# Dilated heads of a hybrid attention layer: gated results written over their gates, and the first head's operands loaded during the phase before

## What is computed

```python
h = layer_norm(x, ln0_g, ln0_b)
proj = jnp.einsum('btd,dc->btc', h, w_in[l])
qa, ka, va, qb, kb, vb, gate = jnp.split(proj, split_at, axis=-1)
ya = dilated_mixture(heads_a(qa), heads_a(ka), heads_a(va), rel_bias).reshape(b, t, WIDTH_A)
yb = stick_breaking(heads_b(qb), heads_b(kb), heads_b(vb)).reshape(b, t, WIDTH_B)
y = jnp.concatenate([ya, yb], axis=-1) * jax.nn.silu(gate)
out = jnp.einsum('btc,cd->btd', y, w_out[l]) + b_out[l]
h = layer_norm(DEEPNORM_ALPHA * h + out, ln_g[l], ln_b[l])
```

## Time and profile before

| what | value |
|---|---|
| median of 3 runs | 1833.44 us |
| the three runs | 1833.44, 1836.2, 1826.37 us |
| profiled execution | 1834.93 us |
| its span in the profile | 1833.1 us |
| TensorE busy | 1706.5 us, 93% |
| VectorE busy | 1173.7 us, 64% |
| ScalarE busy | 806.1 us, 44% |
| GpSimd busy | 194.7 us, 11% |
| mean granted TensorE clock | 0.967 |

### The profile page before, as it was taken

The page is one execution under the profiler, slowest core; times in us unless marked ns, Lnnn a source line. Parts: engine busy times, 40 slices in busy tenths (PEclk is TensorE's granted clock), DMA queues, the critical chain, the costliest instruction groups (busy, mean ns, idle before and its releaser), DMA issues. The chain is left out here.

```text
span 1833.1 us, 27600 instructions
## 1 busy us (share of the span) xinstructions
PE 1706.5 (93%) x9138; PEld 1457.2 (79%) x9138; DVE 1173.7 (64%) x2323; ACT 806.1 (44%) x1993; POOL 194.7 (11%) x172
## 2 busy tenths in 40 slices
PE   5799999999979999999999999959989899959998
PEld 4577888888868888888787888849989899947886
DVE  5531123333238888888888888837667676765996
ACT  3341112222225555555555555538768686742000
POOL 2102100000000000000000000010222222200231
PEclk9899999999989999999999999979989999979999
DMA  4316954666367539465654454259888888446541
GB/s 161 138 66 222 333 193 166 208 200 209 131 188 221 179 124 289 141 179 177 228 178 150 144 157 153 89 140 204 191 213 180 198 183 195 106 135 216 187 151 59
DMA packets 235236, 320.01 MB, mean 175 GB/s; under 512 B 66781, under 2 KB 160408, under 8 KB 231516
## 3 DMA queue, kind: packets, MB, share of 16 engines
q1 hardware_dynamic: 230620, 308.90, 56.5%
q0 software_dynamic: 2400, 9.48, 1.6%
q10 hardware_dynamic: 2080, 0.01, 0.1%
HBM read 208.38 MB, written 109.94 MB: 174 GB/s over the span
## 5 line engine op out<-in xcount | busy, mean ns | idle before, releaser
L1003 ACT ACTIVATE WT_hi<-wt_ps 128x512 fp32r<-128x512 f32 (+1 forms) x320 | 170.9, 534 | 316.3 <-PE wt_ps L935 316.3
L1049 DVE TENSOR_TENSOR_SCAN W<-w,W,zeros 128x512 f32<-128x512 f32 x192 | 248.2, 1293 | 59.3 <-ACT w L995 58.5
L376 PE MATMUL proj<-h_hi,w_hi 128*128 128x512 f32 x640 | 260.2, 407 | 19.2 <-DVE h_lo L552 16.5
L376 PE MATMUL proj<-h_hi,w_lo 128*128 128x512 f32 x640 | 253.2, 396 | 0.0
L376 PE MATMUL proj<-h_lo,w_hi 128*128 128x512 f32 x640 | 252.9, 395 | 0.0
L1358 ACT ACTIVATE prob<-neg_s,rows 128x256 f32<-128x256 f32 (+1 forms) x384 | 173.5, 454 | 51.8 <-DVE rows L1418 47.9
L1057 DVE TENSOR_TENSOR WT_lo<-wt_ps,WT_hi 128x512 fp32r<-128x512 f32 (+1 forms) x320 | 187.4, 586 | 2.2 <-ACT WT_hi L1003 2.2
L1294 PE MATMUL s_ps<-k_both,q_hi 128*128 128x256 f32 (+1 forms) x384 | 151.9, 402 | 38.1 <-DMA q_lo<-qk_lo_d 20.1
L1418 DVE CUSTOM_DVE_ANT_0 neg_s<-s_ps,bias 128x256 f32<-128x256 f32 (+1 forms) x384 | 122.6, 363 | 99.5 <-PE s_ps L1295 89.3
L935 PE MATMUL wt_ps<-ident,W 128*128 128x128 f32 x1088 | 173.5, 275 | 7.0 <-DVE WT_lo L1057 6.2
L995 ACT ACTIVATE w<-z_ps 128x512 f32<-128x512 f32 (+2 forms) x320 | 169.3, 529 | 19.4 <-PE z_ps L925 19.4
(11 more groups left out here) (134 smaller groups left out, 3355.4 us busy)
## 6 DMA issues: line engine op xcount, KB each, us to landing
wa_hi<-wa_d SPq DMA_DIRECT2D x48, 512.0 KB, 3.9
wa_lo<-wa_d SPq DMA_DIRECT2D x48, 512.0 KB, 5.0
va<-va_d SPq DMA_DIRECT2D x32, 512.0 KB, 11.4
wa_d<-x_sb SPq DMA_DIRECT2D x24, 512.0 KB, 3.8
w_raw<-in_w_tiles SPq DMA_DIRECT2D x18, 512.0 KB, 5.1
moved<-move_d SPq DMA_DIRECT2D x16, 528.0 KB, 4.2
x_sb<-in_x SPq DMA_DIRECT2D x16, 512.0 KB, 5.9
qk_hi_d<-st SPq DMA_DIRECT2D x32, 256.0 KB, 2.8
```

What stands on the lines that cost most here:

```text
L376: last = pe.matmul(acc[n % ACC_SLOTS][:], w[w_slot(t)][:, k, :], h[ch][:, k, :], start=(k, a) == (0, 0), stop=(k, a) == (KD - 1, 2))
L1003: act.activation(WT_hi[n % PART_SLOTS][:, cols], t_ps[n % T_SLOTS][:, cols], ACT.Copy) \
L1049: dve.tensor_tensor_scan(W[n % W_SLOTS][:, 0:width][:, ::-1], w[n % W_IN][:, 0:width][:, ::-1], above[:, ::-1], first, ALU.mult, ALU.max). ...
```

## The change

Three things.

1. **Gates.** `apply_gate` writes its product over the gate that it read (`gate`, one tile of 128 x 2048), and the ring `ya_out` is gone, with VectorE's wait on `y_stored`. SP's `finish` stores from `gate`, and now waits until all four stores have landed, before `load_gate` overwrites the tile.
2. **First head.** The tiles of parity 0 of `HeadTiles` (queries, keys, bias) become views of `h_hi[0]` and `h_lo[0]`, for the whole dilated phase. Head 0's queries, keys and bias are loaded in the stick phase: columns 0 to 1535 and the bias at steps 244 and 246, six and eight steps after the last group of chunk 2, and columns 1536 to 2047 at step 281, eight steps after the group of head 0's keys in chunk 3. GpSimd clears the lower half of that `q_lo` in the stick phase as well; the one of parity 1 stays in the dilated phase.
3. **The end of the stick phase.** SP no longer waits there for its stores. It issues head 0's values first in the dilated phase, and waits for the stores after that, before head 1's loads.

```diff
-    def __init__(self, nc, stack):
+    def __init__(self, nc, stack, h_hi, h_lo):
         m = Memory(nc, stack)
-        self.k_both = m.ring("k_both", 2, [P, T], F32R)
...
+        hi, lo = h_hi[:].rearrange("p k c -> p (k c)"), h_lo[:].rearrange("p k c -> p (k c)")
+        self.k_both, self.q_hi2, self.q_lo0 = [hi[:, 0:T]], [hi[:, T:2 * T]], [lo[:, 0:T]]
+        self.bias = [lo[:, T:T + 6 * P].bitcast(F32).rearrange("p (c u) -> p c u", c=3)]
...
+    def set_zeros(self, pool, par):
+        pool.memset(self.q_lo0[par][DH:P, :].bitcast(F32), 0.0).then_inc(self.zeros_set, 1)
...
@@ stick phase, sync
+            def load_first(upto):
+                cols = slice(0, T - CH) if upto < NCH else slice(T - CH, T)
+                stored = A_TILES * (upto - 1) + 4
+                sp.wait_ge(a_done, A_TILES * (NCH - 1))
+                sp.wait_ge(a_stored[stored % 2], a_stored_by(stored))
+                heads.load_qk(sp, qk_hi_d, qk_lo_d, 0, 0, heads.first_loaded, cols)
...
+            plan(A_END[A_TILES * (NCH - 1) - 1] + 6, load_first, NCH - 1)
+            plan(A_END[A_TILES * (NCH - 1) - 1] + 8, load_first_bias)
+            plan(A_END[A_TILES * (NCH - 1) + 4] + 8, load_first, NCH)
...
-            for slot in range(2):
-                sp.wait_ge(y_stored[slot], 16 * GROUPS // 2)
-                sp.wait_ge(a_stored[slot], a_stored_by(A_GROUPS - 2 + slot))
@@ dilated phase, sync
                     sp.dma_start(y_d[bass.ds(pair * P, P), ch * CH:(ch + 1) * CH],
-                                 y_out[ch % 2][:]).then_inc(y_stored[ch % 2], 16)
+                                 gate[:, ch * CH:(ch + 1) * CH]).then_inc(y_stored, 16)
+                sp.wait_ge(y_stored, at(pair, 16 * NCH, 16 * NCH))
...
-            heads.load_dilated(sp, qk_hi_d, qk_lo_d, toe_d, 0, 0)
             load_values(0, 0)
-            heads.load_dilated(sp, qk_hi_d, qk_lo_d, toe_d, 1, 1)
+            for slot in range(2):
+                sp.wait_ge(a_stored[slot], all_stored[slot])
+                sp.wait_ge(b_stored[slot], all_y_stored[slot])
+            heads.load_qk(sp, qk_hi_d, qk_lo_d, 1, 1, qk_loaded[1])
+            heads.load_bias(sp, toe_d, 1, 1)
@@ dilated phase, vector
-                dve.wait_ge(y_stored[ch % 2], at(pair, 16 * NCH // 2, 16 * (ch // 2 + 1)))
-                dve.tensor_tensor(y_out[ch % 2][:], y_ps[ch % 2][:], gate[:, ch * CH:(ch + 1) * CH],
-                                  ALU.mult).then_inc(gated, 1)
+                cols = gate[:, ch * CH:(ch + 1) * CH]
+                dve.tensor_tensor(cols, y_ps[ch % 2][:], cols, ALU.mult).then_inc(gated, 1)
@@ dilated phase, gpsimd
-            for par in range(2):
-                pool.memset(q_lo0[par][DH:P, :].bitcast(F32), 0.0).then_inc(q_zeros_set, 1)
             pool.sem_inc(merged, 1)
+            heads.set_zeros(pool, 1)
```

More of the change, by code:

```diff
@@ L653, in __init__ @@
         self.qk_loaded, self.bias_loaded = m.sems("a_qk_loaded", 2), m.sems("bias_loaded", 2)
[L655 to L665, removed]
+        self.first_loaded, self.zeros_set = m.sem("a_first_loaded"), m.sem("a_q_zeros_set")
@@ new lines, in add_odd, with load_qk @@
+    def add_odd(self, nc, stack):
+        m = Memory(nc, stack)
+        for tiles, name in ((self.k_both, "k_both"), (self.q_hi2, "q_hi2"), (self.q_lo0, "q_lo0")):
+            tiles.append(m.sb(name, [P, T], F32R)[:])
+        self.bias.append(m.sb("bias", [P, 3, 2 * P])[:])
+    def set_zeros(self, pool, par):
+        pool.memset(self.q_lo0[par][DH:P, :].bitcast(F32), 0.0).then_inc(self.zeros_set, 1)
+    def load_qk(self, sp, qk_hi_d, qk_lo_d, head, par, loaded, cols=slice(0, T)):
+        q, k = head * DH, head * DH + WIDTH
+        for tile, half, src, row in ((self.k_both, 0, qk_hi_d, k), (self.k_both, DH, qk_lo_d, k),
+                                     (self.q_hi2, 0, qk_hi_d, q), (self.q_hi2, DH, qk_hi_d, q),
+                                     (self.q_lo0, 0, qk_lo_d, q)):
+            sp.dma_start(tile[par][half:half + DH, cols].bitcast(F32), src[bass.ds(row, DH), cols]) \
+                .then_inc(loaded, 16)
@@ L666, in load_dilated, with load_bias @@
+    def load_bias(self, sp, toe_d, head, par):
         for c in range(3):
@@ L725, in stick_phase @@
     A_END = [next(s for s in range(STEPS) if DEALT[s] >= (a + 1) * KD * 3) for a in range(A_GROUPS)]
+    FIRST_FREE = next(n for n in range(GROUPS) if LAST[n] > A_END[A_TILES * (NCH - 1) - 1])
     def a_group(a):
@@ L844, in store_a, with load_first_bias @@
                     sp.dma_start(gate_d[row:row + P, cols], lo).then_inc(a_stored[a % 2], 16)
+            def load_first(upto):
[4 more added lines that the diff above has]
+                heads.load_qk(sp, qk_hi_d, qk_lo_d, 0, 0, heads.first_loaded, cols)
+            def load_first_bias():
+                heads.load_bias(sp, toe_d, 0, 0)
             later = {}
@@ L906, in _ @@
             for n in range(GROUPS):
+                if n == FIRST_FREE:
+                    pool.wait_ge(a_done, A_TILES * (NCH - 1))
+                    heads.set_zeros(pool, 0)
                 pool.wait_ge(gate_loaded[n % 2], 16 * (n // 2 + 1))
@@ L1090, in _, with dilated_phase @@
                     add_halves(LAST.index(s - VALUES_LAG - 1))
-def dilated_phase(nc, qk_hi_d, qk_lo_d, gate_d, va_d, toe_d, ident, y_d):
+    return [a_stored_by(A_GROUPS - 2 + slot) for slot in range(2)], [16 * GROUPS // 2] * 2
+def dilated_phase(nc, heads, a_stored, all_stored, b_stored, all_y_stored, qk_hi_d, qk_lo_d, gate_d, va_d, toe_d, ident, y_d):
     TURN_HEADS = 2
@@ L1154, in dilated_phase @@
         m = Memory(nc, stack)
-        heads = HeadTiles(nc, stack)
+        heads.add_odd(nc, stack)
         k_both, q_hi2, q_lo0, bias = heads.k_both, heads.q_hi2, heads.q_lo0, heads.bias
@@ L1264, in _ @@
                     sp.wait_ge(rows_done, 2 + at(it, 2 * OBANKS, (par + 1) * OBANKS))
-                    heads.load_dilated(sp, qk_hi_d, qk_lo_d, toe_d, at(it, 2, 2 + par), par)
+                    heads.load_qk(sp, qk_hi_d, qk_lo_d, at(it, 2, 2 + par), par, qk_loaded[par])
+                    heads.load_bias(sp, toe_d, at(it, 2, 2 + par), par)
                     load_values(at(it, 2, 2 + par), par)
@@ L1271, in _ @@
             finish(PAIRS - 1)
-            for i in range(2):
-                sp.wait_ge(y_stored[i], 16 + 16 * PAIRS * NCH // 2)
         @block.tensor
@@ L1284, in scores @@
                 if b % NB == 0:
-                    pe.wait_ge(qk_loaded[par], at(it, 16 * HeadTiles.QK_LOADS, 16 * HeadTiles.QK_LOADS))
+                    first = isinstance(it, int) and it == 0
+                    if first:
+                        pe.wait_ge(heads.zeros_set, par + 1)
+                    if first and par == 0:
+                        pe.wait_ge(heads.first_loaded, 16 * HeadTiles.FIRST_LOADS)
+                    else:
+                        pe.wait_ge(qk_loaded[par], at(it, 16 * HeadTiles.QK_LOADS, 16 * HeadTiles.QK_LOADS * par))
                 pe.wait_ge(min_done, at(it, STEPS, b + 1))
@@ L1795, in build @@
         rstd = stack.enter_context(nc.sbuf_tensor("rstd", [P, TB], F32))
[L1796 to L1804, removed]
```

38 lines of the change are left out of this document (25 added, 13 removed).

## The result

| what | before | changed |
|---|---|---|
| median | 1834.63 us (7 runs) | 1817.92 us (7 runs, 1814.99 to 1825.96) |
| ratio | | 0.9928, 95% interval 0.9912 to 0.9945 |
| profiled execution, its span | 1834.93, 1833.1 us | 1825.96, 1824.1 us |
| mean granted TensorE clock | 0.967 | 0.956 |

The change is faster by 13 us by the ratio and 16.7 by the medians, where 25.5 were forecast. That is the right sign, but between half and two thirds of the size. The median of 1817.9 us lies just inside the range of 1799 to 1819; by the ratio (0.9928 x 1833.4 = 1820 us) it is just outside. The profiled execution is the slowest of the seven; a second profile is with the experiments (e10).

What follows compares the result with a forecast made beforehand. TensorE, busy 93% of the span, was taken as the bound, so only its waits could be won. Start 16.1 plus gatings 9.4 gave 25.5 us off 1834.9, 1809.4 profiled, stated as 1808 us median, range 1799 to 1819.

Steps and rivals of the forecast that it cites:

- The start: Start of the dilated phase: SP's store wait and head 0's loads leave the path, giving 16.1 us.
- the forecast's lower bound: Start of the dilated phase: only 13 us gained if the clock or the order of transfers gives 3 back.
- The moved wait: VectorE's store wait at the gating moves eleven steps on, to the moved rows: 5.0 us at head 2, 4.4 at head 4.
- the 0.8 us of the forecast: SP's chain at the gating: earlier gate load and late stores no longer running against it, together worth 0.8 us.
- The 46.8 us for an undisturbed stretch: Between heads with a gating and no wait: 44.0 us plus some 2.8 for transposes and products.
- the three gatings: Gating of three pairs: 13.3 us won before the clock's charge of 3.9, 9.4 us after it.
- The stick phase: Early loads ahead of group 38's weights: cost 0 within 10 us of slack, 5 us as the other bound.
- I charge 1.3 us behind each of the three moved waits: Lower TensorE clock behind the waits for moved rows: 3.9 us in all, taken from head 0's 1.84 us wait.
- The rule from the Trainium skill: TensorE's lower clock: half the time at it, 3.5 us per wait, 10.5 for three; set aside for 1.3 each.
- All of both waits goes: Rival: SP's chain comes in time, gatings give 26.6 us, total gain 42.7, so 1791 us; chance 0.15.
- Only the start gives: Rival: SP's new wait delays gate load and moves, the clock takes the rest, so 1816 us; chance 0.18.
- The slower rival: SP's wait for all four stores delays each turn; needs a landing 17 us after issue; 1853 us at 20; chance 0.02.

Runs made afterwards that it cites:

- e10: The changed kernel run once more, unaltered, for a second profile: 1822.78 us, ratio 0.9936.
- e2: The changed kernel with the old result ring and old waits for stores, keeping head 0's early loads: 1819.97 us, ratio 0.9921.
- e5: e3 with the loop over turns written out on TensorE, ScalarE and VectorE: 1786.47 us, ratio 0.9747.
- e1: The kernel before with only the gates written over and SP's wait for the four stores: 1843.0 us, ratio 1.0040.
- e6: The changed kernel with the loop over turns written out on TensorE, ScalarE and VectorE: 1820.45 us, ratio 0.9926.
- e7: e5 with eight idle VectorE additions at step 24 of turns 1 to 3, where weigh_maxima stands: 1818.96 us, ratio 0.9922.
- e3: The changed kernel with gate load and SP's wait for stores moved behind head 0's moves in the turn using the gate: 1792.24 us, ratio 0.9759.
- e9: e1 with gate load and SP's wait for stores behind head 0's moves, no early first head: 1803.99 us, ratio 0.9841.
- e8: e5 with eight idle VectorE additions at step 13 of turns 1 to 3, ahead of the gating: 1814.33 us, ratio 0.9886.
- e4: The changed kernel with 24 extra TensorE transposes at step 26 of each turn, result unused: 1823.66 us, ratio 0.9929.

## Why the prediction was right and wrong

*The start: right, with some luck in the number.* First scores came at 1209.9 (1211.1 forecast) and the rows of head 0 were used at 1269.3 (1269.4), 16.3 us against 16.1, behind a wait of 3.0 us. But e10 has 13.1 us at this station, without a wait, and e2 12.8. That is the forecast's lower bound, and its condition, time given back by the clock, is what e10 shows. Counted up to head 1, e10 is 14.4 us ahead and the first profile 11.5.

*The moved wait: right in kind, and mostly in place.* Waits stand at heads 0, 2 and 4 in the first profile (3.0, 4.7, 4.3 us) and at heads 2, 4 and 6 in e10 (5.2, 5.0, 3.9). Forecast were 1.84 us for head 0 and 5.0, 4.4 and about as long for the other three (3.6 for head 6 by the same sum, which the prediction did not work out). So each profile has one fewer than was forecast. From the first store of a pair to the next gate load is 9.6 us, 1340.12 to 1349.73, where it was 10.4: the 0.8 us of the forecast. The 46.8 us for an undisturbed stretch with a gating measured 46.5 to 46.7 in e5, and the three gatings won 13.1 us in e10, where 13.3 were forecast. That writing over an input costs nothing was right as well: the product took 0.691 us before and 0.684 us changed.

*The stick phase: right.* No wait for weights appeared behind the early loads; the only one is that of the first group, 9.6 us (9.5 before).

***"I charge 1.3 us behind each of the three moved waits": wrong.*** This is the term that failed: the price of the clock behind a wait. It came from one wait of 1.84 us with 7 us of half clock behind it. The three moved waits cost 6.7, 6.7 and 4.0 us to the next head in e1, and 6.6, 6.7 and 2.0 in e10, with 24, 24 and 10 us of half clock. So e10 lost 15.3 us where 3.9 were charged. Put into the forecast's sum, that takes 25.5 to 14 us; the profile of e10 has a span 11.7 us shorter than before, since its start gives 14.4 us up to head 1 and not 16.1. In the first profile the stretches behind the waits of heads 2 and 4 lost 3.7 and 5.8. With e10's prices the gatings were worth 13.3 - 15.3 = -2 us, with e1's -4, and not 9.4; that is the sign which e1 shows.

It was a mistake to take one short wait for the price of waits two to three times as long, with two sizes of half clock (7 and 10 us) in view behind the old waits and no row for the new place. But the length of a wait does not set the price either: 3.0 us at head 0 cost 6.1 where 1.84 had cost 1.3, and in e6 6.2 us cost 2.5 where 3.9 cost 6.8. What the loss goes with is how long the clock stays low: 7 us cost 1.0 to 1.3 (before, e6), 10 us 2.0 (e10), 14 us 2.2 to 2.5 (e6, e7), 17 us 3.7 to 4.0, 20 to 24 us 6.1 to 6.8, and the 27 us of e7 7.8. What sets that length stays open.

*A term that the forecast did not have.* The first profile lost more at the start of turn 3, where VectorE stood for 5.9 us and 41 us of half clock followed. It is not in e10, so it belongs to the slowest of the seven runs and does not make the median.

*The rule from the Trainium skill,* in "TensorE: Matmul & The Clock Gate", section Terms (time at the lower clock times one half), would have given 12 us for the 24 us of e1 at half clock; its measured cost was 6.7, as in the first profile the 20.4 us behind head 0 cost 6.1. It overstates the price here by nearly two. But the prediction set it aside for 1.3 us a wait, which was too low by a factor of five at most of these waits. The larger part of that is the length of the half clock (24 us and not 7); the price of a microsecond of it was also higher, 6.7 / 24 = 0.28 us where the row had 1.3 / 7 = 0.19.

*The rivals.* "All of both waits goes" was put at 1791 us for a chain that comes in time. e3 makes it come in time and measures 1792. "Only the start gives", 1816 us, is close to the result by number, but its reason (SP's wait costs more than before) is only half of what happened: the clock did take the rest, while the gate load came no later against the stores. The slower rival asked for landings 17 us after issue; the longest of these stores took 7.5. What e1 shows is that writing over the gates, with SP's wait ahead of the gate load, is slower by itself without any of that, through the clock.

## What to carry to other kernels

When a wait is removed, look for the chain that ends next and for what stands in front of it in its queue. Here the gain came only when a 1 MB load that nobody needed for almost 90 us went behind the transfers that were late, which is one line moved and 26 us. Price a wait of TensorE by the half clock behind it as well as by its length, and as a range: at one and the same place in this kernel, waits of 4 to 6 us were followed by losses of 1 to 7 us. One short wait is no bound for it. Test the halves of a change apart: one of these two halves alone was a loss.

## What the runs showed that was not expected

- The stretch of half clock behind a wait for moved rows was 7 to 24 us, with TensorE at work for nearly all of it, and it varied between profiles of one kernel and between waits of like length. In e9 TensorE was at work for 33 us of half clock at the start of turn 0, where before had 11. Why it lasts is open; e7 and e8 show only that the place matters.
- At the start of turns 2 and 3 VectorE often stands for 2.8 to 6.0 us, with ScalarE beside it for up to 5 where it stands as well, and never at turn 1, which is entered without a jump. All stands of 2.8 to 3.8 us (before, e1, e2, e3, e9, e10) were followed by full clock. Those of 4.9 us and more (e3, whose profile puts it to TensorE, e4 twice, the first profile of the change) were followed by 31 to 41 us of half clock. Written out, the stand is gone. That it is the fetch of code, and that the fetch queues behind the moved rows' small packets, was only argued.
- The fastest kernel is e5, 1786.5 us, 2.5% under before and some 33 us under the change by the ratios.
